# Output tiles innermost in the weight-stationary products of a two-part transformer kernel (one core)

## The reference, cut to what matters

```
T = 256; D = 1024
u = rms_norm(x, attn_norm_w) @ w_in                 # and w_out, peer_w_query
...
a = einsum('thkd,td->thk', down[ib], xb)            # expert scores: 16384 experts x 256 tokens
out = einsum('thk,thkd->td', gate * gelu(a), up[ib])
...
q = h @ xa_q; k = mem @ xa_k                        # second block, also part of its input projection
f = silu(h @ w1) * (h @ w3) @ w2                    # 1024 -> 2816 -> 1024
```

## Time and profile before

| | |
|---|---|
| Median of three runs | 3015.52 us (3012.93, 3015.52, 3020.16) |
| Span of the profiled execution | 3015.1 us |
| PE busy | 2947.5 us, 98% of the span |
| Weight loads (PEld) busy | 2604.2 us, 86% |
| DVE, ACT busy | 67%, 48% |
| DMA | 175 GB/s mean |
| Granted TensorE clock, mean | 0.991 |

### The profile page before, as it was taken

One profiled execution on the slowest core, in us unless ns is written; L12 is line 12 of the kernel. 1 busy time (PEld: TensorE's weight loads), 2 busy tenths in 40 slices (PEclk: granted clock), 3 DMA queues, 4 the chain that ended last, 5 costly groups with the idle time before them and its releaser, 6 DMA issues.

```text
span 3015.1 us, 43968 instructions
## 1 busy us (share of the span) xinstructions
PE 2947.5 (98%) x17320; PEld 2604.2 (86%) x17320; DVE 2016.0 (67%) x3109; ACT 1456.8 (48%) x2275; POOL 14.9 (0%) x37
## 2 busy tenths in 40 slices
PE   8989999999999999999999999999999999999998
PEld 6878888889999788888888999988898998888996
DVE  5859998765555686889885655547665556665554
ACT  5531775554444444157645444435455444545443
POOL 0000000000000000000000000000000000000000
PEclk9999999999999999999999999999999999999999
DMA  5334446775545433444568554546555656554563
GB/s 178 109 113 153 168 168 209 249 268 183 195 178 181 136 99 112 148 163 169 200 224 292 193 196 169 197 141 181 179 171 169 189 187 186 170 182 146 150 187 125
DMA packets 223246, 528.52 MB, mean 175 GB/s; under 512 B 13450, under 2 KB 87344, under 8 KB 212080
## 3 DMA queue, kind: packets, MB, share of 16 engines
q1 hardware_dynamic: 221856, 521.11, 52.1%
q0 software_dynamic: 1232, 5.25, 0.5%
HBM read 507.42 MB, written 18.88 MB: 175 GB/s over the span
## 4 chain that ended last, share of the span: by engine, by line
PE 93%; DVE 4%; ACT 2%; DMA 1%; issue 0%; SPq 0%; POOL 0%; DVEq 0%; ACTq 0%; POOLq 0%
PE ps L2211 16%; PE ps L1232 14%; PE ps L2195 12%; PE ps L1282 12%; PE ps L1295 12%; PE ps L1266 11%; PE ps L559 4%; PE ps L550 3%; PE ps L1221 2%; PE ps L2452 1%; PE ps L653 1%; PE ps L1047 1%; DVE ring_lo L533 0%; PE ps L2376 0%; PE ps L2360 0%; PE ps L1207 0%
## 5 line engine op out<-in xcount | busy, mean ns | idle before, releaser
L1869 DVE TENSOR_TENSOR ring_lo<-ring,w_hi 128x1024 fp32r<-128x1024 f32 x320 | 388.8, 1224 | 272.2 <-ACT w_hi L1865 270.9
L1865 ACT ACTIVATE w_hi<-ring 128x1024 fp32r<-128x1024 f32 x320 | 336.7, 1057 | 270.5 <-PE ps L2211 183.9
L1232 PE MATMUL ps<-h_t,ring 128*128 128x256 f32 x2048 | 463.8, 379 | 1.1 <-ACT arena L882 0.9
L1232 PEld LDWEIGHTS ps<-h_t,ring 128*128 128x128 f32 x2048 | 378.9, 190 | 48.1 <-issue 1.3
L1282 PE MATMUL ps<-h_t_lo,down_hi 128*128 128x256 f32 x1024 | 288.2, 281 | 0.0
L1282 PE MATMUL ps<-h_t_expert,down_lo 128*128 128x256 f32 x1024 | 287.8, 281 | 0.0
L1282 PE MATMUL ps<-h_t_expert,down_hi 128*128 128x256 f32 x1024 | 286.8, 280 | 0.0
L2195 PE MATMUL ps<-h_t_hi,w_hi 128*128 128x256 f32 x928 | 259.9, 280 | 2.7 <-ACT arena L2010 2.7
L2195 PE MATMUL ps<-h_t_lo,w_hi 128*128 128x256 f32 x928 | 261.5, 282 | 0.0
L2195 PE MATMUL ps<-h_t_hi,ring_lo 128*128 128x256 f32 x928 | 259.7, 280 | 0.0
L1656 DVE TENSOR_TENSOR up_lo<-ring,up_hi 128x2048 fp32r<-128x2048 f32 x64 | 146.7, 2292 | 101.4 <-ACT up_hi L945 101.4
(11 more groups left out here) (442 smaller groups left out, 6700.2 us busy)
## 6 DMA issues: line engine op xcount, KB each, us to landing
ring<-in_peer_down SPq DMA_DIRECT2D x128, 1024.0 KB, 5.1
ring<-in_w_in SPq DMA_DIRECT2D x140, 512.0 KB, 3.6
ring<-in_peer_up SPq DMA_DIRECT2D x68, 1024.0 KB, 4.8
ring<-in_w SPq DMA_DIRECT2D x132, 512.0 KB, 3.7
ring<-in_peer_up SPq DMA_DIRECT2D x120, 512.0 KB, 4.1
arena<-late_gates SPq DMA_DIRECT2D x16, 1024.0 KB, 7.0
ring<-in_w_out SPq DMA_DIRECT2D x16, 512.0 KB, 3.5
ring<-in_peer_w_query SPq DMA_DIRECT2D x16, 512.0 KB, 3.5
```

What stands on the lines that cost most here:

```text
L1232: m = pe.e.matmul(PS[:, act_bank(b), j * T:(j + 1) * T], RING[:, b % 2, j * D + kc * P:j * D + (kc + 1) * P], HT[:, kc, :], start=kc == 0, ...
L1865: a.e.activation(W_HI[:, g % HI_SLOTS, :], RAW[:, g % RAW_SLOTS, :], ACT.Copy).then_inc(*a.count(f"c{g}_hi"))
L1869: v.e.tensor_tensor(RAW_LO[:, g % RAW_SLOTS, :], RAW[:, g % RAW_SLOTS, :], W_HI[:, g % HI_SLOTS, :].bitcast(F32), ALU.subtract).then_inc(* ...
```

## The change

In the three weight-stationary functions the loop over output tiles (`c`, `j`) moves from outermost to innermost. Before, one output tile was completed (over all `kc` and the three passes) before the next was begun. Now each step of `kc` and pass is done for all output tiles of the chunk before the next step. Neighbouring matmuls so have the same moving tokens, and write different column ranges of a bank. In `act_in_parts` the `start` flag, which opens an accumulation in a bank, is now set on the first matmul of the bank alone, as it already was in the other two.

```
 front_chunk, j in (0, 4, 5, 10, 11):
-                for c in range(-(-w // P)):
-                    cw = min(P, w - c * P)
-                    for kc in range(k):
-                        for i, (y, z) in enumerate(((hi, x[0]), (hi, x[1]), (lo, x[0]))):
+                for kc in range(k):
+                    for i, (y, z) in enumerate(((hi, x[0]), (hi, x[1]), (lo, x[0]))):
+                        for c in range(-(-w // P)):
+                            cw = min(P, w - c * P)
                             m = pe.e.matmul(PS[0:cw, 2 * (j % 2) + c // 2, (c % 2) * T:(c % 2 + 1) * T],
...
 act_in_parts:
-                for j in range(2):
-                    for kc in range(KD):
-                        o = slice(j * D + kc * P, j * D + (kc + 1) * P)
-                        passes = ((DOWN_HI, HT_EXPERT), (DOWN_HI, HT_LO), (DOWN_LO, HT_EXPERT))
-                        for n, (w, x) in enumerate(passes):
+                for kc in range(KD):
+                    passes = ((DOWN_HI, HT_EXPERT), (DOWN_HI, HT_LO), (DOWN_LO, HT_EXPERT))
+                    for n, (w, x) in enumerate(passes):
+                        for j in range(2):
+                            o = slice(j * D + kc * P, j * D + (kc + 1) * P)
                             m = pe.e.matmul(PS[:, 4 + b, j * T:(j + 1) * T], w[:, b, o], x[:, kc, :],
-                                            start=kc == 0 and n == 0, stop=kc == KD - 1 and n == 2)
+                                            start=kc == 0 and n == 0 and j == 0, stop=kc == KD - 1 and n == 2,
+                                            skip_group_check=True)
...
 channels:
-                for c in range(2):
-                    for kc in range(4):
-                        for i, (w, y) in enumerate(((hi, x[0]), (hi, x[1]), (lo, x[0]))):
+                for kc in range(4):
+                    for i, (w, y) in enumerate(((hi, x[0]), (hi, x[1]), (lo, x[0]))):
+                        for c in range(2):
```

## The result

The changed kernel takes 3024.07 us (median of 10 runs, 3020.64 to 3027.86); the kernel before takes 3015.3 us in the runs beside it. The ratio is 1.0026, with an interval of 1.0017 to 1.0034: slower, by 8.8 us between the medians, 8.5 us between the means and 7.9 us by the ratio. Forecast was no change, at 3015.5 us; the range ended at 3025.0 and so holds the median, but the change is clear of the noise and none was forecast.

What follows compares the result with a forecast made beforehand. PE's own rate was taken as the bound, PE being busy 98% of the span. Three terms at 0 ns on 7200 products summed to 0 us, so 3015.5 us was forecast, range 3005 to 3025 us.

Steps and rivals of the forecast that it cites:

- The count and the bound: 7200 matmuls in L1282, L2195 and L550 change order, none added or removed; PE's own rate bounds the dense stretches.
- (c): All changed products: weight tiles always alternate, where hi weights were loaded twice running; price 0.
- goes one for one into the time: Expert loop and second block's feed-forward, PE never idle: any change in matmul spacing adds its own length to the time.
- (a): Changed products write another half of the bank each time, in place of the same half; price 0.
- (b): Changed products stream the same moving tokens twice or four times in a row; price 0.
- The rival of 38 us: Shared tokens cheaper in the rounded type: 3820 products save 10 ns each, giving 2977 us; chance 0.07.
- the estimate of 2951 us: Spacing rule gives 109.2 ns for 256 columns; if the old order caused the excess, about 64 us lower.
- a rival at 6 ns and one in three: New pairings of streamed and loaded tiles stall: 2400 changed products at 6 ns, 14.4 us, 3030 us; chance 0.14.
- The sign that I had named for it: In the changed kernel's profile, steps of 0.12 and 0.13 us alternating in a pattern that repeats with kc.
- the mean of 118 ns: L1282 and L2195, 6240 products at 117.8 and 118.1 ns: taken to show no such stall loss.
- the 0.84 ns that I had asked for: Spacing change per product needed to be told from no change: 6.0 us over 7200 products.

Runs made afterwards that it cites:

- act_pass_inner: Kernel before with kc outermost, then j, then the three passes in act_in_parts; ratio 1.0004, 11.147 us for 48 + 24 products.
- act_banks: Kernel before with act_in_parts alone in the new order, each output in a bank of its own; ratio 1.0015, 11.193 us for 48 + 24 products.
- act_halves_unshared: Kernel before with j innermost in act_in_parts, j = 1 four kc ahead, so no neighbours share tokens; ratio 1.0019, 11.193 us for 48 + 24 products.
- act_weights_in_turn: Kernel before with second and third pass of act_in_parts exchanged, j still outermost; ratio 0.9995, 11.113 us for 48 + 24 products.
- pad_short: Kernel before with three identical float32 products added at the end of each layer's expert loop; ratio 1.0022, +5.5 us.
- the pads: Kernel before with three, or in a second run six, identical float32 products added after each layer's expert loop; ratios 1.0022 and 1.0019.
- act_only: Kernel before with only act_in_parts in the new order; ratio 1.0022, +6.1 us, 11.193 us for 48 + 24 products.

## Why the prediction was wrong

**The count and the bound were right.** PE's rate is the bound in the dense stretches; 7200 products; no wait was added, and ACT's wait for L1282 is 250.9 us (246.4 in the earlier trace rows). Two steps failed: the term (c), put at 0, and the sentence that the spacing "goes one for one into the time".

**(a) Halves of a bank, price 0: right.** act_pass_inner and the long stretch of `channels` (127.23 against 127.20 us) show it with accumulating products, which the gate sums were not, and act_banks shows that banks of their own are worth nothing.

**(b) Shared tokens, price 0: right.** act_halves_unshared takes them away and changes nothing; act_weights_in_turn adds them and loses nothing. The rival of 38 us, and the estimate of 2951 us by the rule of N / 2.4 + 2.5 ns (the Trainium skill, TensorE: Matmul & The Clock Gate, "Wait — 56ns, not 53.3ns?"), have nothing in the runs for them: the products still take 118 to 119 ns, in every order of the expert loop that ran.

**(c) "Another sequence of weight tiles ... Price taken: 0" is the first step that failed.** It measured 0.046 us for 72 products, 2.9 us in all: 0.6 ns for each of the 3072 of L1282 (5.70 / 48 against 5.67 / 48), and the rest on L1295, which I had left out because nothing in it changes. With 0.5 us in `channels` and 0.5 in `front_chunk` it is 3.9 us. I had seen the stall in L550 and made it a rival at 6 ns and one in three; the mechanism of that rival, that some pairings of streamed and loaded tile come late, fits what the runs show, its size was off (3.9 us in place of 14.4), and it works on the call behind as well. The sign that I had named for it, a pattern that repeats with kc, is in the changed trace: from the starts of L1282, averaged over its calls, the steps repeat every six products, which is one kc, as 118, 119, 117, 122, 115, 123 ns. Before, they run through a longer pattern of 15. I took the mean of 118 ns over many buffers as a sign that nearly all orders are free. It was only a sign that the orders in use were. By itself this loss, 3.9 / 7200 = 0.54 ns per product, lies under the 0.84 ns that I had asked for, and might have gone unseen.

**"One for one into the time" is the second: a term was missing, the clock.** Of the 8.8 us some 3 to 4 go with a mean granted clock of 0.9895. The mean of the 110 later executions of the kernel before is 0.9908, which makes it 3.1 us; the runs of the kernel before beside the result have no clock on record, but were faster than those 110 (3015.9 against 3017.1 us), which by the same 2.4 us for 0.001 makes it 0.9913 and 4.3 us, an estimate. With 3.9 us of spacing that is 7.0 to 8.2 of the 8.5 us between the means; the rest is within the scatter. I had treated a gain or loss in a dense stretch as worth its own length. pad_short shows that it is not: 2.6 us of neutral work cost 5.5. The low clock is found in and just behind the short stages in which PE is idle in part: in the kernel before PE is busy for 9.28 of 14.00 us from 143 us on, and the 5 us behind that have a clock of 0.66. In none of the 16 traces is it found in the expert loops or in the dense stretches of the earlier trace rows. Which of the short stages are caught differs from trace to trace.

**The account:** `act_in_parts` 6.1 us, of which 2.9 spacing and about 3 clock; `front_chunk` 3.0 us, of which 0.5 is spacing and about 2 go with the clock; `channels` 0.2 us, where its trace has 0.5. The spacing is shown by the traces of kernels that differ in the order alone. That the clock takes its share is shown for the shift by the pads; for `front_chunk` it rests on how time goes with the clock.

**What stays open.** Why two neighbours from the same two buffers cost 0.6 ns in `act_in_parts` and, with `mt_hi` and `mt_lo`, 1.3 ns in `channels`, but nothing with `h_t_hi` and `h_t_lo`; and why the first products of L1295 are slow: 231 ns on average for the first seven before, 232 for the first ten in the changed kernel, and 227 ns for all that follow in both. Nor is it shown why a shift of one or two us moves the mean clock of ten executions, and not only that of a single one. That it depends on the buffers speaks for their places in memory; no run moved a buffer, so this is only argued. A cause that no run tested is also the engine's supply of instructions.

**A version that beats both** is not established: act_weights_in_turn saves 64 x 0.034 = 2.2 us in the expert loop by its trace, and measures 0.9995 (0.9986 to 1.0005), which can't be told from no change. It is a gain over the changed kernel.

## What to carry to other kernels

Where the matrix engine is busy 98% of the time with thousands of like products, a reordering that "moves nothing" can still be worth a fraction of a nanosecond per product, and that is to be priced from the sequence of buffers, for just these buffers, and not from a mean over others. Read it from starts that lie many calls apart, since all calls agree to 0.003 us, while the total scatters by several us. And a shift of one or two us before stages with partial idling can cost or give back as much again by the clock; test for it with a neutral pad before a small difference is put down to the edit, and don't compare half-clock stretches between two single executions.

## What the runs showed of the hardware

- The spacing of rounded products with 256 columns in the expert loop is 118.0 to 119.2 ns, depending on the sequence of the buffers they stream and load; the bank, the half of the bank, shared tokens and the kc order have no effect (11.147 us in the kernel before and act_pass_inner, 11.193 us in act_only, act_banks and act_halves_unshared).
- The order of one call moves the time of the next, unchanged one: 24 products of 512 columns take 5.45, 5.46, 5.47, 5.48 or 5.49 us after different orders of the 48 before them, and the difference is in the first ten.
- 0.001 of mean granted clock goes with 2.4 us in this kernel, and neutral work of 1.3 us per layer moved the mean clock by 0.0017; twice as much by 0.0006.
